# Weights loaded and divided in blocks of 128x512 through six buffers in place of 128x1024 through three

## Time and profile before

| | us |
|---|---|
| Median of 3 runs | 2650.56 |
| Lowest, highest | 2649.93, 2665.92 |
| Profiled execution | 2650.76 |
| Its span, first to last instruction | 2648.9 |
| TensorE busy in it | 2485.6 |
| VectorE busy | 1212.5 |
| ScalarE busy | 919.8 |
| GpSimd busy | 407.4 |

### The profile page before, as it was taken

How to read it: one execution, slowest core, us unless ns; L and a number is a source line. 1 busy time by engine, 2 the same in 40 slices (tenths; PEclk the granted TensorE clock), 3 DMA queues, 4 the chain that set the end, 5 groups by cost and what they waited for, 6 DMA issues and landing times.

```text
span 2648.9 us, 51461 instructions
## 1 busy us (share of the span) xinstructions
PE 2485.6 (94%) x22813; PEld 2339.3 (88%) x22813; DVE 1212.5 (46%) x1982; ACT 919.8 (35%) x1215; POOL 407.4 (15%) x584
## 2 busy tenths in 40 slices
PE   8899999999999999899999998999999969999996
PEld 7898888888889998789999988888889969998996
DVE  6553554535544553532243344466545553233332
ACT  5413343233333344332232241333335453233222
POOL 2101011110100101011111111122212212111111
PEclk9999999999999999999999999999999979999998
DMA  9333333233333544543333333443444445333322
GB/s 241 107 92 91 99 99 100 84 91 91 103 107 99 153 140 116 161 158 88 88 88 89 88 128 98 111 115 112 119 120 122 137 126 161 88 87 83 87 79 77
DMA packets 378862, 292.94 MB, mean 111 GB/s; under 512 B 20295, under 2 KB 342609, under 8 KB 378104
## 3 DMA queue, kind: packets, MB, share of 16 engines
q1 hardware_dynamic: 336272, 172.51, 24.0%
q0 software_dynamic: 24944, 83.64, 9.8%
q10 hardware_dynamic: 17424, 33.50, 3.5%
HBM read 231.10 MB, written 59.23 MB: 110 GB/s over the span
## 4 chain that ended last, share of the span: by engine, by line
PE 78%; DVE 7%; ACT 6%; DMA 4%; issue 4%; POOL 0%; ACTq 0%; SPq 0%; DVEq 0%; POOLq 0%
PE psd L541 62%; PE psw L564 2%; PE psw L563 2%; PE psw L584 1%; DVE w_lo L1634 1%; ACT w_hi L1099 1%; PE psw L612 1%; PE psw L569 1%; PE psw L634 1%; DVE arena L1735 1%; DMA w_raw<-in_ab_w_in_dram 1%; DMA raws<-uT_scratch 1%; DMA uT_scratch<-mix 1%; PE psw L620 1%; DMA mix<-in_x_prompt_dram 1%
## 5 line engine op out<-in xcount | busy, mean ns | idle before, releaser
L541 PE MATMUL psd<-xh,w_hi 128*128 128x272 f32 x5056 | 1118.7, 303 | 46.7 <-DVE xl L1686 13.4
L541 PE MATMUL psd<-xh,w_lo 128*128 128x272 f32 x5056 | 1055.6, 290 | 2.0 <-issue 2.0
L541 PE MATMUL psd<-xl,w_hi 128*128 128x272 f32 x5056 | 1054.9, 290 | 0.5 <-issue 0.5
L541 PEld LDWEIGHTS psd<-xh,w_hi 128*128 128x128 f32 x5056 | 805.3, 191 | 107.6 <-issue 45.6
L541 PEld LDWEIGHTS psd<-xl,w_hi 128*128 128x128 f32 x5056 | 806.3, 191 | 0.0
L541 PEld LDWEIGHTS psd<-xh,w_lo 128*128 128x128 f32 x5056 | 801.3, 191 | 2.7 <-issue 2.7
L1634 DVE TENSOR_TENSOR w_lo<-w_raw,w_hi 128x1024 fp32r<-128x1024 f32 x316 | 388.3, 1231 | 583.6 <-ACT w_hi L1099 582.1
L1099 ACT CAST w_hi<-w_raw 128x1024 fp32r<-128x1024 f32 x316 | 328.8, 1043 | 772.9 <-PE psd L541 741.5
L2445 POOL TENSOR_TENSOR states<-states,extra 128x544 f32<-128x544 f32 x59 | 98.5, 1670 | 562.9 <-ACT extra L1154 562.9
L2386 POOL DMA_DIRECT2D raws<-uT_scratch x61 | 38.1, 625 | 775.9 <-DMA uT_scratch<-mix 686.4
L2267 DVE TENSOR_TENSOR extra<-psd,rstd 128x544 f32<-128x544 f32 x32 | 23.2, 724 | 143.2 <-PE psd L541 112.7
(11 more groups left out here) (499 smaller groups left out, 2331.4 us busy)
## 6 DMA issues: line engine op xcount, KB each, us to landing
w_raw<-in_ab_w_in_dram SPq DMA_DIRECT2D x112, 512.0 KB, 4.0
w_raw<-in_cd_w_in_dram SPq DMA_DIRECT2D x74, 512.0 KB, 4.1
w_raw<-in_ple_w_gate_dram SPq DMA_DIRECT2D x64, 512.0 KB, 3.9
uT_scratch<-mix ACTq DMA_DIRECT2D x92, 272.0 KB, 4.3
w_raw<-in_ab_w_out_dram SPq DMA_DIRECT2D x32, 512.0 KB, 3.9
w_raw<-in_cd_w_out_dram SPq DMA_DIRECT2D x32, 512.0 KB, 3.9
raws<-uT_scratch POOLq DMA_DIRECT2D x40, 272.0 KB, 3.1
hT_scratch<-arena POOLq DMA_DIRECT2D x2, 4352.0 KB, 19.0
```

The costliest lines, as they stand in the source:

```text
L541: mm = pe.matmul(out[:, D0 + HALF * half:D0 + HALF * (half + 1)], w[:, r, k % KH, :], x[:, k, HALF * half:HALF * (half + 1)], start=(k == ...
```

## The change

The weights go through the kernel in quarters of a tile in place of halves: four slices (512 rows, 256 KB) a block, 632 blocks, and six buffers of half the size in place of three. The memory for w_raw, w_hi and w_lo stays as large as it was. SPLITS now places the division of block q at slice number 4(q-4), again sixteen slices ahead of its use, and it waits for the block six back. Every division is one instruction on ScalarE and one on VectorE as before, over 512 columns. TensorE waits for w_lo at every fourth slice. At the start the input loads x3 and x4 stand behind two quarters, and three divisions stand at c == 4, 6 and 8.

```diff
-        NW = 3
-        w_raw = sb("w_raw", [P, NW, KH, P])
-        w_hi, w_lo = sb("w_hi", [P, NW, KH, P], F32R), sb("w_lo", [P, NW, KH, P], F32R)
+        QH, NW = KT // 4, 6
+        NQ = KT // QH
+        w_raw = sb("w_raw", [P, NW, QH, P])
+        w_hi, w_lo = sb("w_hi", [P, NW, QH, P], F32R), sb("w_lo", [P, NW, QH, P], F32R)
...
-        def half_end(q):
-            return POS[q // 2, KH * (q % 2) + KH - 1] + 1
+        def quarter_end(q):
+            return POS[q // NQ, QH * (q % NQ) + QH - 1] + 1
...
-        for q in range(2, NSL // KH):
-            SPLITS.setdefault(max(KH * (q - 2), half_end(q - NW) if q >= NW else 0), []).append(q)
+        for q in range(NQ, NSL // QH):
+            SPLITS.setdefault(max(QH * (q - NQ), quarter_end(q - NW) if q >= NW else 0), []).append(q)
...
-            for q in range(2 * len(TILES)):
-                if q == 1:
+            for q in range(NQ * len(TILES)):
+                if q == 2:
                     load_x(3)
                     load_x(4)
...
-                    src = W_DRAM[name][layer, 1024 * (q % 2):1024 * (q % 2) + 1024, c:c + width]
+                    src = W_DRAM[name][layer, P * QH * (q % NQ):P * QH * (q % NQ + 1), c:c + width]
...
-                q = 2 * d + k // KH
+                q = NQ * d + k // QH
...
-                if k % KH == 0:
+                if k % QH == 0:
                     pe.wait_ge(S["lo_ready"], q + 1)
...
-                    act.wait_ge(S["slice_done"], half_end(q - NW))
+                    act.wait_ge(S["slice_done"], quarter_end(q - NW))
                 act.copy(w_hi[:, q % NW], w_raw[:, q % NW]).then_inc(S["hi_ready"], 1)
...
-                if c == 4:
-                    split_lo(1)
+                if c in (4, 6, 8):
+                    split_lo(c // 2 - 1)
```

More of the change, by code:

```diff
@@ L180, in group_table @@
     return order
-SEMS = """w_landed0 w_landed1 w_landed2 hi_ready lo_ready slice_done dense_read0 dense_read1 stage_stored0 stage_stored1
+SEMS = """w_landed0 w_landed1 w_landed2 w_landed3 w_landed4 w_landed5 hi_ready lo_ready slice_done dense_read0 dense_read1 stage_stored0 stage_stored1
 act_chain dve_chain pool_chain work_ready in_copied nrm_sq nrm_ln nrm_rstd x_hi x_ready y_done h_loaded0 h_loaded1 h_loaded2 h_loaded3 z_loaded dn_z gl_z sp_z sq_added sq_summed
@@ L490, in _ @@
                 load_x(t)
-            for q in range(2 * len(TILES)):
-                if q == 1:
+            for q in range(NQ * len(TILES)):
+                if q == 2:
                     load_x(3)
                     load_x(4)
-                name, layer, starts, *_ = TILES[q // 2]
+                name, layer, starts, *_ = TILES[q // NQ]
                 if q >= NW:
@@ L514, in _ @@
             sp.wait_ge(S["y_stored0"], 16 * (NT + 2))
[L516 to L519, removed]
+        landed, count = [], [0] * NW
+        for q in range(NQ * len(TILES)):
+            count[q % NW] += 16 * len(TILES[q // NQ][2])
+            landed.append(count[q % NW])
         @block.tensor
@@ L540, in dense_slice @@
                     for half in range(2):
-                        mm = pe.matmul(out[:, D0 + HALF * half:D0 + HALF * (half + 1)], w[:, r, k % KH, :],
+                        mm = pe.matmul(out[:, D0 + HALF * half:D0 + HALF * (half + 1)], w[:, r, k % QH, :],
                                        x[:, k, HALF * half:HALF * (half + 1)],
@@ L1548, in _ @@
             for c in range(KT):
-                if c == 4:
-                    split_hi(1)
+                if c in (4, 6, 8):
+                    split_hi(c // 2 - 1)
                 if c == 10:
```

## The result

The changed kernel takes 2633.9 us (median of 7 runs, 2625.1 to 2640.9); the kernel before takes 2657.8 us in the runs beside it (7 runs, 2649.3 to 2665.9). The ratio is 0.9916, 95% interval 0.9899 to 0.9932. The profiled execution after took 2638.2 us (span 2636.4). Against the 2650.8 and 2648.9 of before it is 12.6 us shorter in the span, half of what the medians say: the executions of one kernel differ by up to 17 us, and the mean granted clock differs with them (0.970 to 0.977 after, 0.966 to 0.972 before).

The account below looks back on a forecast made before the run. The prediction took TensorE, busy 94% of the span, as the bound, with only its idle time to win. Its terms, -2.2 - 2.9 + 2.5 + 1.9 - 1.0 = -1.7 us against 2650.8, gave 2649.1 us, range 2638 to 2661.

Parts of the forecast that it names:

- the heads' term: Delta heads, 125 to 776 us: closed gaps -2.8, shorter divisions in chains -5.0, new divisions in chains +6.8; -1.0 us.
- The three that I had put down to the late release: Heads: three gaps of 0.66, 0.85 and 1.27 us over a division's two steps, said to go with earlier release.
- Short divisions before TensorE goes on: Five places from the start to output projection 1: shorter division directly before TensorE resumes, less one new division; -2.2 us.
- The rows chain: Start: a quarter landing 2.1 us sooner and its shorter division advance beta and decay rows, cutting TensorE's idle; -2.9 us.
- The early starving: Start: TensorE starves at slice 60, not 64, while VectorE is in the rows, but waits for the same chain anyway.
- No load wait at 58: Start, a sign to look for: ScalarE no longer waits there for a weight load; the wait before was 2.96 us.
- The layer-1 rows: Rows of layer 1: shorter divisions give 0.9 us and the earlier starving takes it back; 0.
- The look-ahead: Divided weights run out sooner: +2.5 us at layer 1's B/C conv, +1.9 at output projection 1.
- Price of a division: Every division: 512 columns take 0.62 us on ScalarE and 0.69 on VectorE, from a line through the 544 and 1024 times.
- A slice: TensorE: a slice stays at 12.03/16 = 0.752 us, already fulfilled extra waits costing nothing.
- Faster by little: Rival: no new division in a head's chain, no wait at the start, no dry places; 2637 us, chance 0.12.
- Faster clearly: Rival: under 2624 us, needing a sixth of TensorE's whole idle time of 163 us to go; chance 0.04.

Follow-up runs that it names:

- e1: The changed kernel, but each division waits for the block five back, not six, so the engines stand there until TensorE comes; 2632.5 us, ratio 0.9920.
- e10: The changed kernel with divisions run three to five slices further before layer 1's B/C conv, norm rows and output projection, and layer 0's rows; 2623.8 us, ratio 0.9882.
- e9: The kernel of e6, but the first division of a pair also waits until TensorE reaches the slice where it stands; 2643.6 us, ratio 0.9958.
- e3: The changed kernel with weights loaded in 512 KB blocks again, one load for two quarters; 2640.0 us, ratio 0.9945.
- e5: The kernel before, each division as two instructions of 512 columns, the second four slices behind the first on ScalarE and VectorE; 2644.0 us, ratio 0.9955.
- e8: The kernel before, with divisions as two instructions of 512 columns four slices apart on VectorE alone; ScalarE keeps its 1024; 2644.5 us, ratio 0.9961.
- e4: The kernel before, each division written as two instructions of 512 columns at the same place on both engines; 2647.0 us, ratio 0.9976.
- e7: The kernel before with 99 unneeded matmuls added at 34 places of the heads where TensorE stood idle; 2649.9 us, ratio 0.9973.
- e11: The kernel of e2 with 209 unneeded matmuls added at 14 places where TensorE had long idle gaps; 2615.9 us, ratio 0.9855.
- e6: The changed kernel, but divisions stand in pairs, two after one another every eight slices; 2634.8 us, ratio 0.9925.
- e2: The changed kernel, but each quarter is divided twenty slices ahead of its use in place of sixteen; 2632.0 us, ratio 0.9915.

## Why the prediction was wrong

**The step that failed is the heads' term.** I had -1.0 us, with bounds -8 and +7; the profile shows -13.9. My sign for being wrong was that the idle time there moves by more than 8 us; it moved by 5.4, so the sign stayed silent, as it looked at idle time alone. Two things were wrong in the term.
- *TensorE's busy time was taken as fixed.* "Only its idle time can be won" is false here: 8.5 of the 13.9 us are the same matmuls at a higher clock. Rows 2 showed 0.98 in the heads and 0.81 to 0.92 around the long waits, and I read these numbers without pricing them. The sum had no line for what an idle gap costs after it has ended.
- *The idle time moved by -5.4, not -1.0, because the gains were priced too low.* Matmul by matmul, nine waits of these slices are longer after, by 6.5 us together, close to the +6.8 that I had for new divisions (0.81 became 1.36 in head 2). Not each of them is a new division: one of 0.37 us in head 4 became 1.36 because before, at 1.2 GHz, TensorE's own matmuls had filled that wait. All other waits together fell by about 12 us, where I had -7.8. Those with a division in the chain fell by the difference of one, as priced: 1.47 to 1.03 on ScalarE, 1.79 to 1.25 on VectorE (head 5). But others went whole, where the sum had half a microsecond at most for such a wait; what ended the longest the trace doesn't name. TensorE before, where the wait after is 0.00:

```profile
653.86 0.65 PE L584 MATMUL psw<-arena 32*32 32x32 f32 x32 [1.99 <-issue]
```

The three that I had put down to the late release went from 0.66, 0.85 and 1.27 to 0.00, 0.00 and 0.16, but e1 shows the same with the late release kept: that part of the mechanism was wrong, and the number right by luck.

**Short divisions before TensorE goes on, -2.2:** right where the trace lets it be seen. Start -0.56 (0.54 expected), output projection 8.56 to 7.71 us of idle, which is 0.85 (0.74), gate tile 0.54.

**The rows chain, -2.9:** too large. The early starving came, longer than I had it; timeline of TensorE after:

```profile
74.21 0.52 PE L542 MATMUL psd<-xh,w_hi 128*128 128x272 f32 x2 [2.21 <-DVE w_lo L1635]
...
84.29 0.82 PE L542 MATMUL psd<-xh,w_hi 128*128 128x272 f32 x2 [3.81 <-DVE w_lo L1635]
...
116.95 1.19 PE L564 MATMUL psw<-arena,ones 128*128 128x256 f32 x2 [2.75 <-ACT arena L1222]
```

8.8 us of idle in place of 4.36 and 5.78; slice 95 starts 1.0 us earlier, the 0.56 of the start among them. "No load wait at 58" failed too: ScalarE still waited there, 2.34 us until 59.26. The load came when I had said, but the quarter before it had come late as well.

**The layer-1 rows, put at 0:** too small. Slices 1424 to 1504 took 78.9 us in place of 77.1, with two new waits for w_lo in them, 0.63 and 2.10 us; the loss was there and the gain of 0.9 did not cover it.

**The look-ahead, +2.5 and +1.9:** TensorE did stop four slices sooner at the conv, but for 7.27 us, not 12. The conv itself began 2.1 us sooner behind the evacuation (its first operation 9.2 us after the evacuation's start, 11.3 before, the difference being the way through the scratch buffer in DRAM), and over slices 1478 to 1531 the kernel gained 1.9 us. The price of the missing look-ahead was right all the same: e10 took it away and got 3.1 us back. At output projection 1 the new wait for w_lo was 1.29 us, not 2.7, and the 1.17 behind it went as said. Of each of these terms the loss was there; it was hidden in the sum by gains I had not seen.

**Price of a division:** 0.615 and 0.714 us against 0.62 and 0.69. The Trainium skill (VectorE: DVE Perf Modes, "The TRN2 errata") gives an estimate of 691 ns; the mean here is 714, and 694 in e9. Its rule that small tiles pay the fixed cost again holds here: the two engines are busy 81 us longer in all. That this speaks against the change was my reading, and it was wrong: the slice of the dense stretches, below, is no longer for it.

**A slice** still costs 12.03/16 us, and the added waits nothing. The chain of the kernel after:

```profile
1386.52 12.03 PE psd L542 x96
```

**The rivals.** "Faster by little" (2637, chance 0.12) had the right sign and the nearest number, but for the wrong reason: it left out the new divisions in the chains and the dry places, both of which are there, so the near number is luck. "Faster clearly" (under 2624) was not reached either. I had argued against it by how much idle time would have to go; the clock is a way to gain that this argument left out.

**What is shown and what is not.** Shown: in the profiled executions the gain lies in the heads, in every kernel that has it; it needs neither small loads (e3) nor six buffers (e5, e8) nor early release when the divisions are single (e1); shorter instructions at one place bring a third of it at most (e4); the clock follows TensorE's idle time (e7, e11). That about half of the gain is clock rests on one pair of profiles in the heads and, for the whole kernel, on the estimate from spans and clocks above. Open: why pairs of divisions keep it when the first may start early (e6). The times of e9 speak for the length of division left when TensorE arrives, its profile does not. One profiled execution for each kernel is also too few to say how much of 28.9 us at the low clock is chance; that the nine kernels whose profiles have the shorter heads without added matmuls show 0.0 to 12.0 there, and the two that lack it 24.2 and 28.9, says that not all is.

## What to carry to other kernels

- Work for a stream that shares its engines with a latency-bound chain can be worth cutting small and setting apart, even where the total grows: here each wait fell by what the piece in its way had become shorter (1.47 to 1.03 us, 1.79 to 1.25).
- Price an idle gap of the busiest engine with what follows it. Read the granted clock in the stretch behind each gap; where it is low, shortening the gap can give back more than the gap, and filling it with matmuls that nobody needs gives time back too (16 us here, in e11).
- When the pieces of a stream get smaller, look at every place that relied on the last large piece for its look-ahead, and lengthen it there.

## What the runs showed of the hardware

- In the trace of before, gaps of TensorE of 1.47 and 1.27 us were followed by 3.4 and 6.8 us at 1.2 GHz; with the one of 7.72 us in e2 went 13.7, a part of it within the gap. Not each gap was followed: before, one of 1.47 and one of 1.79 us were not, and after the change six of 1.24 to 1.36 us in the heads were not. What decides was not measured.
- The clock is a good part of what differs between executions of one kernel: after the change the spans ran from 2623.3 us at a mean clock of 0.977 to 2639.1 at 0.970.
- Two rounding copies of 512 columns back to back took 1.13 us, one of 1024 1.04; two subtractions 1.29 against 1.23 (e4 and before). Splitting as such cost 0.06 to 0.09 us there.
